# u-row gathers and dot products moved from the U stage of the expert layer into its V stage

## What is computed

```python
q = (xb @ wq).reshape(-1, PEER_HEADS, 2, half)              # 8 heads, two halves
s1, s2 = einsum(q[:, :, 0], k1), einsum(q[:, :, 1], k2)       # 128 keys each
...                                                           # top 16 of each, then of their sums
idx = take_along_axis(cidx, pos, axis=-1)                     # 16 of 16384 experts per head
gw  = softmax(sc)
act = gelu(einsum('thkd,td->thk', take(u, idx, axis=0), xb))  # dot with row u[idx]
y   = einsum('thk,thkd->td', gw * act, take(v, idx, axis=0))  # weighted sum of rows v[idx]
```

## Time and profile before

| | |
|---|---|
| median of three timed runs | 2498.86 us (2486.26, 2498.86, 2500.0) |
| profiled execution | 2486.21 us, span 2484.4 us |
| mean granted clock of TensorE | 0.947 |
| TensorE busy | 2305.5 us, 93% |
| VectorE, ScalarE, POOL busy | 1523.3, 1234.5, 1073.5 us |
| U stages (first to last matmul) | 418.4 to 797.9 us, 1639.8 to 2019.5 us |
| V stages | 887 to 1250 us, 2107 to 2469 us |
| moved by DMA | 455.49 MB, mean 183 GB/s |

### The profile page before, as it was taken

One profiled execution on the slowest core, in us unless ns is written; L12 is line 12 of the kernel. 1 busy time (PEld: TensorE's weight loads), 2 busy tenths in 40 slices (PEclk: granted clock), 3 DMA queues, 4 the chain that ended last, 5 costly groups with the idle time before them and its releaser, 6 DMA issues. The chain is left out here.

```text
span 2484.4 us, 58392 instructions
## 1 busy us (share of the span) xinstructions
PE 2305.5 (93%) x20464; PEld 2091.6 (84%) x20484; DVE 1523.3 (61%) x3131; ACT 1234.5 (50%) x2355; POOL 1073.5 (43%) x1000
## 2 busy tenths in 40 slices
PE   5966999999999999999979679999999999999998
PEld 4943777999998889999979238689999987999997
DVE  3466634993553976776554756359645459676765
ACT  3530113557545965555544302145674469555554
POOL 0004102885675844444200141058757767444431
PEclk8966899999999999999989688999999999999999
DMA  7556123555885057777444560345568830777763
GB/s 267 166 172 215 57 87 125 181 178 199 283 295 187 0 186 245 253 247 238 158 154 156 189 216 3 111 153 178 183 230 281 294 102 21 258 246 253 249 214 104
DMA packets 123816, 455.49 MB, mean 183 GB/s; under 512 B 13744, under 2 KB 14256, under 8 KB 122544
## 3 DMA queue, kind: packets, MB, share of 16 engines
q1 hardware_dynamic: 105264, 386.80, 44.2%
q0 software_dynamic: 18432, 67.12, 10.4%
HBM read 449.37 MB, written 4.49 MB: 183 GB/s over the span
## 5 line engine op out<-in xcount | busy, mean ns | idle before, releaser
L402 POOL TENSOR_TENSOR parts<-ring,parts 128x512 fp32r<-128x512 f32 x358 | 488.4, 1367 | 399.9 <-ACT parts L395 383.7
L395 ACT ACTIVATE parts<-ring 128x512 fp32r<-128x512 f32 x616 | 385.9, 631 | 387.0 <-PE ps_u L449 219.1
L445 PE MATMUL ps_u<-h_parts,parts 128*128 128x256 f32 x4096 | 566.1, 280 | 5.8 <-ACT parts L395 5.1
L2536 PE MATMUL ps_y<-act_parts,parts 128*128 128x256 f32 x4096 | 562.0, 280 | 0.0
L445 PEld LDWEIGHTS ps_u<-h_parts,parts 128*128 128x128 f32 x4096 | 516.1, 188 | 10.1 <-ACT parts L395 8.6
L2536 PEld LDWEIGHTS ps_y<-act_parts,parts 128*128 128x128 f32 x4096 | 515.1, 188 | 0.7 <-ACT parts L2484 0.3
L2582 POOL TENSOR_TENSOR act_parts<-big,act_parts 128x256 fp32r<-128x256 f32 x256 | 216.3, 845 | 422.6 <-ACT act_parts L2565 422.6
L402 DVE TENSOR_TENSOR parts<-ring,parts 128x512 fp32r<-128x512 f32 x258 | 184.8, 718 | 339.2 <-ACT parts L395 196.3
L449 PE MATMUL ps_u<-h_parts,parts 128*128 128x256 f32 x2048 | 328.4, 282 | 7.5 <-POOL parts L402 5.0
L2540 PE MATMUL ps_y<-act_parts,parts 128*128 128x256 f32 x2048 | 321.6, 279 | 0.0
L449 PEld LDWEIGHTS ps_u<-h_parts,parts 128*128 128x128 f32 x2048 | 276.2, 189 | 16.7 <-POOL parts L402 14.4
(11 more groups left out here) (388 smaller groups left out, 2859.2 us busy)
## 6 DMA issues: line engine op xcount, KB each, us to landing
ring<-in_stream SPq DMA_DIRECT2D x570, 512.0 KB, 3.6
more_ring<-in_stream SPq DMA_DIRECT2D x126, 512.0 KB, 3.7
big<-in_stream SPq DMA_DIRECT2D x16, 512.0 KB, 12.2
out_state_out<-big SPq DMA_DIRECT2D x2, 1440.0 KB, 7.0
big<-in_state SPq DMA_DIRECT2D x2, 1280.0 KB, 11.2
big<-in_mixc SPq DMA_DIRECT2D x2, 1024.0 KB, 8.5
big<-in_spots SPq DMA_DIRECT2D x2, 1024.0 KB, 5.3
x_res<-in_x SPq DMA_DIRECT2D x1, 1152.0 KB, 5.4
```

The costliest lines, as they stand in the source:

```text
L395: eng.activation(m.parts[:, q % PARTS, 0, :], half_tile(m, t, half), ACT.Copy).then_inc(s["hi_ready"], 1)
L402: eng.tensor_tensor(m.parts[:, q % PARTS, 1, :], half_tile(m, t, half), m.parts[:, q % PARTS, 0, :].bitcast(F32), ALU.subtract).then_inc(m ...
L445: pe.matmul(out, hi[:, k, :], hr[:, side, kk, 0:tokens], start=(kk + side == 0), stop=False)
L2536: pe.matmul(ps[:, half * KD // 2 + k, :], hi[:, k, :], act_parts[:, j % AHEAD, side, :], start=False, stop=False)
```

## The change

All 32 u-row gathers and dots of a layer leave `experts_block` and go into `combine_block`. There a turn of six tiles now holds twice as many: two rows for every three tiles. Turn 0 stays plain. Turns 1 to 8 carry the gathers and dots, each dot behind the second and the third of three tiles; turn 9 carries none (the Gelu of the dots stands ahead of it on ScalarE, the multiplication with the gates behind it on VectorE); turns 10 to 17 carry the v-row gathers and the weighted sums at the same places. Both use the two buffers `m.rows`, and `dot_rows` is gone. The core of the diff:

```diff
 def experts_block(...):
-            each_tile(act, TURNED + RING, DOTS_END + RING, tile)
-            act.wait_ge(s["dots_ready"], 1)
-            act.activation(m.dot, m.dot, ACT.Gelu_apprx_tanh).then_inc(s["dots_out"], 1)
-            each_tile(act, DOTS_END + RING, NKEYS - 2, tile)
+            each_tile(act, TURNED + RING, NKEYS - 2, tile)
...
-            for turn in range(DOTS // RING - 1, DOTS_END // RING):
...
-            each_tile(pool, DOTS_END, NKEYS, first_half)
+            each_tile(pool, TOPK_TILES, NKEYS, first_half)
...
-            each_tile(v, DOTS, DOTS_END, dot)
-            for q in range(2):
-                v.wait_ge(s[f"row_used{q}"], HALF)
-            v.sem_inc(s["dots_ready"], 1)
-            v.memset(m.tokens, 0.0)
...
+            each_tile(v, SOFT + 2 * RING, NKEYS, second_half)
 def combine_block(...):
-    ADD = 1
+    DOT = 1
+    DOT_END = DOT + HALF // 2
+    ADD = DOT_END + 1
+    ADD_END = ADD + HALF // 2
...
-            each_tile(act, 0, NKEYS, tile, VRING)
+            each_tile(act, 0, VRING * DOT_END, tile, VRING)
+            act.wait_ge(s["dots_ready"], 1)
+            act.activation(m.dot, m.dot, ACT.Gelu_apprx_tanh).then_inc(s["act_ready"], 1)
+            each_tile(act, VRING * DOT_END, NKEYS, tile, VRING)
...
+            def fetch(table, index, n, q):
+
+                used = n if table is u_rows else HALF + n
+                if used:
+                    pool.wait_ge(s[f"row_used{q}"], used)
...
+            for turn in range(2 * TURNS):
+                for j in range(RING):
+                    tile(turn // 2, turn % 2 * RING + j)
+                    for table, index, at in ((u_rows, m.u_row, 2 * DOT), (v_rows, m.v_row, 2 * ADD)):
+                        if j == 0 and 0 <= turn - at < HALF:
+                            fetch(table, index, turn - at, 1)
+                        if j == 2 and 0 <= turn + 1 - at < HALF:
+                            fetch(table, index, turn + 1 - at, 0)
...
+            def tile_dot(g, j):
+                tile(g, j)
+                if j % RING:
+                    q, n = j % RING - 1, (g - DOT) * 2 + j // RING
+                    fetched(q, n)
+                    v.scalar_tensor_tensor(m.rows[:, q, :], m.rows[:, q, :], 1.0, m.tokens, ALU.mult, ALU.mult,
+                                           accum_out=m.dot[:, ds(n * 2 + q, 1)]).then_inc(s[f"row_used{q}"], 1)
...
+            each_tile(v, VRING * DOT, VRING * DOT_END, tile_dot, VRING)
+            for q in range(2):
+                v.wait_ge(s[f"row_used{q}"], HALF)
+            v.sem_inc(s["dots_ready"], 1)
+            v.memset(m.tokens, 0.0).then_inc(s["weighted"], 1)
+            each_tile(v, VRING * DOT_END, VRING * ADD, tile, VRING)
+            v.wait_ge(s["act_ready"], 1)
+            v.tensor_tensor(m.dot, m.dot, m.weight, ALU.mult).then_inc(s["weighted"], 1)
+            v.wait_ge(s["weighted"], 2)
+            each_tile(v, VRING * ADD, VRING * ADD_END, tile_add, VRING)
```

More of the change, by code:

```diff
@@ L2445, in _, with combine_block @@
                 weigh(TURNS - 1, g)
-def combine_block(nc, m, l, stream):
+def combine_block(nc, m, l, stream, u_rows):
     AHEAD = 2
@@ L2585, in _ @@
             v_rows = stream.rearrange("l t p d -> (l t p) d")
-            def fetch(n, q):
-                if n:
-                    pool.wait_ge(s[f"row_used{q}"], n + q)
-                pool.indirect_dma_start(m.rows[:, q, :], None, v_rows,
-                                        bass.IndirectOffsetOnAxis(ap=m.v_row[:, 2 * n + q:2 * n + q + 1], axis=0)).then_inc(
-                    m.fetched[q], 16)
-            for turn in range(TURNS):
-                n = turn - ADD
-                for j in range(VRING):
-                    tile(turn, j)
-                    if j == 0 and 0 <= n < HALF:
-                        fetch(n, 1)
-                    if j == 3 and 0 <= n + 1 < HALF:
-                        fetch(n + 1, 0)
+            def fetch(table, index, n, q):
+                used = n if table is u_rows else HALF + n
+                if used:
+                    pool.wait_ge(s[f"row_used{q}"], used)
+                pool.indirect_dma_start(m.rows[:, q, :], None, table,
+                                        bass.IndirectOffsetOnAxis(ap=index[:, 2 * n + q:2 * n + q + 1], axis=0)).then_inc(
+                    m.fetched[q], 16)
+            for turn in range(2 * TURNS):
[6 more added lines that the diff above has]
+                            fetch(table, index, turn + 1 - at, 0)
             each_tile(pool, VRING * TURNS, NKEYS, tile, VRING)
@@ L2622, in tile_add @@
                     else:
[L2623 removed]
+                        v.wait_ge(s["row_used1"], n + HALF)
                     v.scalar_tensor_tensor(m.tokens, m.rows[:, q, :], m.dot[:, ds(n * 2 + q, 1)], m.tokens,
                                            ALU.mult, ALU.add).then_inc(s[f"row_used{q}"], 1)
[L2627 to L2629 removed]
+            each_tile(v, 0, VRING * DOT, tile, VRING)
@@ L2630, in _ @@
+            each_tile(v, VRING * ADD, VRING * ADD_END, tile_add, VRING)
+            v.wait_ge(s["row_used1"], 2 * HALF)
             v.sem_inc(s["samples_ready"], 1)
-            each_tile(v, VRING * (ADD + HALF), VRING * (TURNS - 1), tile, VRING)
+            each_tile(v, VRING * ADD_END, VRING * (TURNS - 1), tile, VRING)
             v.wait_ge(s["samples_summed"], 1)
@@ L2676, in build @@
                 output_block(nc, m, l, hr, stream, small_out, state_out)
-                experts_block(nc, m, l, hr, stream, spots_in, u_rows)
+                experts_block(nc, m, l, hr, stream, spots_in)
             gates_block(nc, m, l)
-            combine_block(nc, m, l, stream)
+            combine_block(nc, m, l, stream, u_rows)
             clear(nc, m.loaded + m.done)
```

55 lines of the change are left out of this document (10 added, 45 removed).

## The result

The changed kernel is slower: a median of 2502.1 us (2492.4 to 2510.2, 22 runs) against 2488.9 us for the kernel before (2479.1 to 2506.1, 22 runs), a ratio of 1.0042 with a 95% interval of 1.0026 to 1.0058. The ratio makes it 10 us more, the two medians 13. I had forecast 16 us less.

What follows compares the result with a forecast made beforehand. TensorE, busy 93% of the span, was taken as the bound. A U-stage gain of 24 us minus 2 x (3.5 + 0.6) = 8 us of V-stage cost gave 16 us less: 2476 us predicted, range 2460 to 2502.

Steps and rivals of the forecast that it cites:

- What the U stage gives back: U stages: without gathers and dots TensorE regains nearly full pace, 24 us less over both layers, bounds 20 and 25.
- VectorE and POOL fit into 8.40 us: V stage: two tiles with a dot and one without take 8.22 of 8.40 us, so TensorE is not held.
- Rival 2: V stage: VectorE and POOL become the bound at 8.89 us per turn, 31 us lost, net 7 slower; chance 0.16.
- The stream's tiles cost nothing with six slots: V stage: six slots give a tile 14 us to land, so late tiles cost nothing.
- Rival 1: V stage: the DMA limit moves along, costing 50 us against 24 gained, 26 us slower, 2512; chance 0.14.
- The gathers: V stage: some 27 us of waits for gathers, three quarters absorbed by margin; 3.5 us per layer, ends 0 and 12.
- Rival 3: V stage: slow gathers pile up to 12 us per layer, about no change, 2487; chance 0.14.
- The Gelu: V stage, between dots and sums: ScalarE waits for the last dot, 0.6 us per layer, ends 0 and 3.
- The sum: Whole kernel: 8 us of V-stage cost against 24 us of U-stage gain, 16 us less.
- The two groups of executions: Timed runs of the kernel before: one at 2486.3, two at 2499 to 2500 us, taken as groups 13 us apart.

Runs made afterwards that it cites:

- four buffers: Changed kernel with four row buffers instead of two, each gather issued four tiles ahead: 2466.7 us against 2487.1 for the kernel before, ratio 0.9914.
- half tiles: Changed kernel with V-stage stream tiles of 256 KB from the second turn on, gathers whole: 2468.6 us beside 2487.1 for the kernel before.
- half rows: Changed kernel with equally many gathers of 2 KB instead of 4 KB per partition: 2463.0 us.
- no gathers: Changed kernel with 62 of 64 gathers per layer left out, dots and sums kept on old data: 2471.5 us beside 2485.2 for the kernel before.

## Why the prediction was wrong

- **What the U stage gives back:** right. 26.6 us against 24 forecast, with full pace in the old window and ScalarE's wait for tiles gone. The reading by matmul counts held. The upper bound of 25 was a little low.
- **VectorE and POOL fit into 8.40 us:** right. They do at full load, by the four buffers. That the spare is small, 0.2 us by the forecast, is worked out and was not measured. Rival 2 (lone lengths on the shared port, 8.89 us) didn't happen.
- **The stream's tiles cost nothing with six slots:** right. No V stage showed a wait for them. Rival 1 didn't happen, at 311 GB/s.
- **The gathers:** this is the step that failed: "With 128 gathers the same rate would make some 27 us of waits, of which the margin should take three quarters", and with it the term of "3.5 us per layer". Both factors were wrong. The rate did not stay the same: 50 of 128 gathers took over 7 us, not 18 of 128, and VectorE's waits for them were 60.0 us, not 27. And the margin took half of it, not three quarters: TensorE's loss without the Gelu's was 18.8 us in layer 0 (21.6 - 2.8) and 12.3 in layer 1 (14.5 - 2.2), 31.1 of 60.0. The ends of 0 and 12 per layer were too narrow. The median gather was in time as forecast, at 5.4 us with 6.3 to land (5.0 to 5.1 and 6.6 forecast); a median says nothing of how many lie beyond the margin. Rival 3, slow gathers piling up, was the nearest, at a price of 12 us per layer where 12 to 19 was due, and had 0.14.
- **The kernel before as evidence:** the share of late gathers was taken from a U stage whose TensorE was itself held up (1180 matmuls in 150 us instead of 1287), and from a V stage with its gathers 8.4 us apart. I took the tiles' lateness as cured by depth, which was right, and the share of late gathers as fixed, though tiles and gathers go through the same DMA engines. The half tiles and the half rows show that this share depends on the traffic beside a gather. That the three slots of the U stage held the stream back and so kept gathers in time is likely, and not shown by a run of its own.
- **The Gelu:** 2.8 and 2.2 us against 0.6, since the last dot was late as well. With gathers on time it costs 0.0 to 0.2 (no gathers, half rows, four buffers), so the mechanism was sized too high for its own case, and its end of 3 for the late case was about right.
- **The sum:** 26.6 - 36.1 instead of 24 - 8. Of the 28 us by which the cost was too low, the gathers are 24 (31.1 instead of 7) and the Gelu 4 (5.0 instead of 1.2).
- **The two groups of executions** 13 us apart, which the forecast's range rests on, were chance in three times: the 22 executions of the kernel before spread from 2479 to 2506 us, over half of them at 2484 to 2491. This didn't decide anything.

Not shown: what the last parts of a late gather wait behind. The experiments tell the conditions under which late gathers become frequent, pairs of them and a full stream, and not the order of service inside the DMA engines.

## What to carry to other kernels

A landing time is a property of the traffic around a transfer, not of the transfer, and it has a tail: here 18 of 128 took over 7 us with a median near 5, and denser traffic made 50 of them without moving the median much. Before a change that shortens the time to land (for the v rows from 14.8 us to 6.3 here), count the landings beyond the new margin, expect more of them where the traffic is denser, and ask what a late one costs the engine that all wait for. Then give the transfers depth (four row buffers here, 0.9914) or spread their issues (0.9953). An engine whose chain of work fills 8.22 of 8.40 us works as long as nothing it waits for is late; look for the slack in the buffers ahead of it before moving work to it.

## What was not expected of the hardware

In some spells three tiles take 8.48 us and not 8.40, at the same clock, with TensorE busy throughout. Two windows of the timed four-buffer kernel, in the dot turns and the sum turns of layer 0:

```profile
900.00:1020.00 120.00, 120.00 (x1022) 120.00 (x1021) 103.13 (x142) 66.72 (x127) 73.76 (x69) 1.00 0.89 308
1060.00:1180.00 120.00, 120.00 (x1031) 120.00 (x1030) 104.35 (x114) 67.46 (x129) 75.04 (x67) 1.00 0.87 302
```

1022 matmuls in 120 us against 1031, at clock 1.00 in both. In layer 1 of the same execution it is the other way round, and in the other profile of this kernel layer 1 has it in both. A stage of it costs 3 us. The load of the DMA engines isn't what brings it: with halved tiles, layer 0 ran at 8.48 and layer 1 at 8.40. Its cause is open.
